# Modulation vectors of a diffusion block: VectorE multiply-adds on raw weight slabs in place of split slabs and TensorE row products

## What is computed

```
def adaln(cvec, w, b):                        # w: (1024, 6144), b: (6144,)
    m = silu(cvec) @ w + b
    return split(m, 6)                        # shift1, scale1, gate1, shift2, scale2, gate2

layer 0:  sh1, sc1, g1, sh2, sc2, g2 = adaln(c, ada_w[0], ada_b[0])        # and the same with c_ctx for t
          x += g1 * ab_mixer(rmsnorm(x) * (1 + sc1) + sh1)                 # also t
          x += g2 * swiglu(rmsnorm(x) * (1 + sc2) + sh2)                   # also t, D_FF 2816
layer 1:  the same six vectors from ada_w[1]; for t only the first two are used
          x += g1 * attention(...)            # 16 heads of two kinds, 512 keys
          x += g2 * top2_of_8_experts(...)
out = rmsnorm(x) * final_gain
```

## Time and profile before

| | |
|---|---|
| median of 3 runs | 1918.21 us (1916.23 to 1924.85) |
| profiled execution, own time | 1920.28 us |
| its span | 1918.5 us |
| mean granted TensorE clock | 0.956 |
| PE busy / DVE busy / ACT busy | 1770.2 / 1314.5 / 994.5 us |
| slabs loaded in all / of the modulation matrices | 401 split / 48 |
| moved by DMA | 426.31 MB |

### The profile page before, as it was taken

How to read it: one execution, slowest core, us unless ns; L and a number is a source line. 1 busy time by engine, 2 the same in 40 slices (tenths; PEclk the granted TensorE clock), 3 DMA queues, 4 the chain that set the end, 5 groups by cost and what they waited for, 6 DMA issues and landing times.

```text
span 1918.5 us, 23197 instructions
## 1 busy us (share of the span) xinstructions
PE 1770.2 (92%) x8673; PEld 1411.3 (74%) x8674; DVE 1314.5 (69%) x1238; ACT 994.5 (52%) x884; POOL 10.1 (1%) x24
## 2 busy tenths in 40 slices
PE   5899978999999977899769999999999999999995
PEld 2676657888888767555658888888878887888884
DVE  5536545453535555788449798889888888888896
ACT  5444324212221153544247777777777777777674
POOL 0000000000000000000000000000000000000000
PEclk9889989999999978899869999999999999999998
DMA  9446422232232222344129999999999999999992
GB/s 354 169 156 214 153 88 71 105 117 80 87 109 72 74 91 88 110 132 143 55 86 351 341 356 335 345 335 360 339 343 348 342 352 336 361 330 356 344 354 108
DMA packets 215147, 426.31 MB, mean 222 GB/s; under 512 B 8806, under 2 KB 64648, under 8 KB 215052
## 3 DMA queue, kind: packets, MB, share of 16 engines
q1 hardware_dynamic: 210178, 420.33, 63.0%
q10 hardware_dynamic: 4234, 4.57, 0.8%
q0 software_dynamic: 640, 0.04, 0.0%
HBM read 423.86 MB, written 1.05 MB: 221 GB/s over the span
## 4 chain that ended last, share of the span: by engine, by line
PE 81%; DVE 9%; ACT 5%; issue 3%; DMA 1%; SPq 1%; DVEq 0%; ACTq 0%
PE bank L478 25%; PE bank L480 24%; PE bank L479 24%; DVE lo L428 4%; ACT hi L422 3%; PE bank L1814 2%; PE bank L1853 1%; PE bank L1516 1%; DMA raw<-in_ada_w_dram 1%; PE bank L1517 1%; DVE rowmax L1278 1%; DVE mrow L1294 1%; PE bank L1887 0%; PE bank L1507 0%; PE bank L1888 0%
## 5 line engine op out<-in xcount | busy, mean ns | idle before, releaser
L428 DVE TENSOR_TENSOR lo<-raw,hi 128x2048 fp32r<-128x2048 f32 x401 | 910.8, 2282 | 301.6 <-ACT hi L422 299.8
L422 ACT ACTIVATE hi<-raw 128x2048 fp32r<-128x2048 f32 x401 | 763.9, 1910 | 495.7 <-PE bank L480 482.5
L478 PE MATMUL bank<-hi,xgh 128*128 128x512 f32 (+1 forms) x864 | 328.9, 381 | 9.9 <-DVE lo L428 6.3
L479 PE MATMUL bank<-lo,xgh 128*128 128x512 f32 (+1 forms) x864 | 325.2, 376 | 0.0
L480 PE MATMUL bank<-hi,xgl 128*128 128x512 f32 (+1 forms) x864 | 325.1, 376 | 0.0
L478 PEld LDWEIGHTS bank<-hi,xgh 128*128 128x128 f32 x864 | 163.0, 189 | 42.8 <-DVE lo L428 6.5
L480 PEld LDWEIGHTS bank<-hi,xgl 128*128 128x128 f32 x864 | 162.7, 188 | 33.0
L479 PEld LDWEIGHTS bank<-lo,xgh 128*128 128x128 f32 x864 | 162.8, 188 | 31.3
L478 PE MATMUL bank<-hi,aTh 128*128 128x512 f32 x396 | 159.1, 402 | 0.0
L480 PE MATMUL bank<-hi,aTl 128*128 128x512 f32 x396 | 154.8, 391 | 0.0
L479 PE MATMUL bank<-lo,aTh 128*128 128x512 f32 x396 | 154.3, 390 | 0.0
(11 more groups left out here) (315 smaller groups left out, 2314.2 us busy)
## 6 DMA issues: line engine op xcount, KB each, us to landing
raw<-in_moe_w_gate_dram SPq DMA_DIRECT2D x99, 1024.0 KB, 5.5
raw<-in_moe_w_up_dram SPq DMA_DIRECT2D x99, 1024.0 KB, 5.6
raw<-in_moe_w_down_dram SPq DMA_DIRECT2D x99, 1024.0 KB, 5.5
raw<-in_ada_w_dram SPq DMA_DIRECT2D x48, 1024.0 KB, 6.1
raw<-in_ffn_w_gate_dram SPq DMA_DIRECT2D x11, 1024.0 KB, 5.3
raw<-in_ffn_w_up_dram SPq DMA_DIRECT2D x11, 1024.0 KB, 5.5
raw<-in_ffn_w_down_dram SPq DMA_DIRECT2D x11, 1024.0 KB, 6.1
raw<-in_ab_w_in_dram SPq DMA_DIRECT2D x6, 1024.0 KB, 6.4
```

The costliest lines, as they stand in the source:

```text
L422: nc.scalar.activation(hi[n0 % SPL][:, 0:size], raw[slot][:, 0:size], ACT.Copy).then_inc(hi_ready, 1)
L428: nc.vector.tensor_tensor(lo[n0 % SPL][:, 0:size], raw[slot][:, 0:size], hi[n0 % SPL][:, 0:size].bitcast(F32), ALU.subtract).then_inc(lo_r ...
L478: nc.tensor.matmul(dst, lh, rh, start=first, stop=False, skip_group_check=True)
L479: nc.tensor.matmul(dst, lh, rl, start=False, stop=False, skip_group_check=True)
```

## The change

Blocks 0 to 3 of layer 0 stay as they were. The other 20 blocks (40 slabs) are no longer split. DVE reads the raw slab itself: for each of its 4 pieces and each conditioning vector it does one `scalar_tensor_tensor` of 128x512 (weights times a per-partition number, plus the sum so far) into `acc`; the bias lies in partition 0 of a cleared tile `biased`, which SP now loads, and stands in for the sum in the first operation. Layer 1's blocks 4 to 11 have one vector; their 4 operations go in two alternating sums, added at the end of the block. TensorE then only sums over partitions (`spread`): `acc` as weight and a column of ones for a column block (8 or 4 matmuls of one column), or ones as weight and 512 columns of `acc` for a gate row. The operations on DVE are placed by `MIX_STEPS` (input projection), beside the output projection, and by `FFN_BLOCKS`: one or two blocks in each feed-forward step, whose loop is now written out. None is left in the attention. GpSimd's queue is empty.

```diff
+MIX_STEPS = [[(4, 0)], [(4, 1), (5, 0)], [(5, 1)], [(6, 0), (6, 1)], [(7, 0)], [(7, 1)]]
 for j_ in range(6):
-    MIX_SLABS += [("ab_in", j_)] + [("ada0", (4 + j_, h)) for h in range(2)]
-MIX_SLABS += [("ada0", (cb, h)) for cb in (10, 11) for h in range(2)]
-MIX_SLABS += [("ada1", (cb, h)) for cb in (0, 1) for h in range(2)]
-MIX_SLABS += [("ab_out", (h, q)) for h in range(2) for q in range(2)]
-MIX_SLABS += [("ada1", (cb, h)) for cb in (2, 3) for h in range(2)]
+    MIX_SLABS += [("ab_in", j_)] + [("ada0", key) for key in MIX_STEPS[j_]]
+for h_ in range(2):
+    MIX_SLABS += [("ab_out", (h_, q)) for q in range(2)] + [("ada0", (8 + h_, q)) for q in range(2)]
+FFN_BLOCKS = [[]] + [[(0, 10)], [(0, 11)], [(1, 0)], [(1, 1)], [(1, 2)], [(1, 3)], [(1, 6), (1, 7)], [(1, 8), (1, 9)],
+                     [(1, 4), (1, 5)], [(1, 10), (1, 11)]]
...
+            def direct(layer, cb, h):
...
+                ops = [(k, who, who) for k in range(4) for who in range(2)] if pair else [(k, 0, k % 2) for k in range(4)]
+                for i, (k, who, part) in enumerate(ops):
+                    w_, c_ = raw[slot][:, 512 * k:512 * k + 512], cs[:, 8 * who + 4 * h + k:8 * who + 4 * h + k + 1]
+                    sum_ = acc[:, place_, part, :]
+                    if i >= 2 or h:
+                        chain.wait(1 if i else 0)
...
+                        ins = V.scalar_tensor_tensor(out=sum_, in0=w_, scalar=c_,
+                                                     in1=biased[:, place_, :] if h == 0 and i < 2 else sum_,
+                                                     op0=ALU.mult, op1=ALU.add)
...
             for j in range(6):
                 project("ab_in", [(j, 256)], 8, range(4), tok(Hhi, Hlo), lambda t: (j, t), None if j else h_ready[0])
-                rows_of_block(0, 4 + j)
-                if j >= 1:
-                    columns_of(0, 3 + j)
...
+                if j in (2, 3):
+                    spread(0, 2 + j)
...
+                for layer, cb in FFN_BLOCKS[i]:
+                    for h in range(2):
+                        direct(layer, cb, h)
+                hidden(i, i % 2)
...
+                    if b_ == 0 and kind == "g" and i >= 2:
+                        for layer, cb in FFN_BLOCKS[i - 1]:
+                            spread(layer, cb)
...
-                if i % 4 == 0 and i >= 4:
-                    columns_of(1, late_block(i - 4))
-                if i < 32 and i % 2 == 0:
-                    rows_of(1, late_block(i - i % 4), i % 4 // 2)
```

More of the change, by code:

```diff
@@ L97, in bank_order @@
     out.append(("start", 1, [("cT", 0)]))
[L98 to L101, removed]
+    for cb in range(4):
+        out.append(("ada0", 1, [(("m", cb), 5 + cb % 2, (cb, 1)), (("col", cb), 7)]))
+    out.append(("ada0", 1, [(("bc", cb, who), 5 + who) for cb in (4, 5) for who in range(2)] + [(("col", cb), b) for cb, b in ((6, 7), (7, 5), (8, 6), (9, 7))]))
     out.append(("norm0", 1, [(k, k % 5) for k in range(8)]))
@@ L207, in mark, with wait @@
         self.n += 1
[L209 to L218, removed]
+    def wait(self, back=0):
+        self.eng.wait_ge(self.sem, self.n - back)
 def build(nc, a, out):
-    slabs, n, landed = {}, 0, [0] * RAW
+    slabs, splits_made, directs_made, landed, held = {}, 0, 0, [0] * RAW, []
     for stage, times, keys in slab_order():
@@ L616, in _ @@
             load(sp, "ukv", 0, columns(a["d_w_ukv"][0], slice(0, 2), 0, D))
-            for cb in LATE:
-                for h in range(2):
-                    ada(1, (cb, h))
             for h in range(2):
@@ L834, in _ @@
                             "uq", (h, a_))
-            for stage, key in LATE_SLABS[0:2]:
-                splits(stage, key)
+            splits(*LAST_SLABS[0])
             for t in range(NT):
@@ L1053, in _ @@
                         emptied(V.tensor_copy(zp[:, t, (j - 4) * 256:(j - 3) * 256], b[:, 0:256]), "ab_in", (j, t))
-                mix(3 * j + 3, 3 * j + 6)
-                mod_row(0, 4 + j)
-                if j >= 1 and 3 + j not in GATE_BLOCKS:
-                    mod_col(0, 3 + j)
+                if j < 5:
+                    splits("ab_in", j + 1)
+                for cb, h in MIX_STEPS[j]:
+                    direct(0, cb, h)
                 if j == 3:
@@ L1506, in columns_of @@
                 for j in range(4):
[L1507 removed]
+                    for who in range(2 if in_pair(layer, cb) else 1):
+                        ins = T.matmul(b[:, 2 * j + who:2 * j + who + 1], sums[:, who, j * P:(j + 1) * P], ones[:, 0:1],
+                                       start=True, stop=True)
                 filled(ins, st, ("col", cb))
[L1510 to L1522 removed]
             def norm(i):
@@ L1666, in _ @@
-            hidden("u", "ffn_out", "u9", 9)
-            down("ffn_out", "d8", 8, 0)
-            hidden("g", "ffn_out", "g10", 10)
-            hidden("u", "ffn_out", "u10", 10)
-            down("ffn_out", "d9", 9, 1)
-            down("ffn_out", "d10", 10, 0)
+            hidden("g", 0)
+            hidden("u", 0)
+            hidden("g", 1)
+            for i in range(1, FFI):
+                hidden("u", i)
+                down(i - 1)
+                if i + 1 < FFI:
+                    hidden("g", i + 1)
@@ L1673, in _ @@
+            down(FFI - 1)
+            for layer, cb in FFN_BLOCKS[FFI - 1]:
+                spread(layer, cb)
             norm(2)
```

498 lines of the change are left out of this document (238 added, 260 removed).

## The result

| | before | changed kernel |
|---|---|---|
| median | 1920.13 us (1916.23 to 1924.85, 4 runs) | 1878.57 us (1875.79 to 1881.64, 4 runs) |
| ratio of the two | | 0.978, 95% interval 0.977 to 0.980 |
| profiled execution / its span | 1920.28 / 1918.5 us | 1878.65 / 1876.4 us |
| mean granted clock | 0.956 | 0.937 |
| PE / DVE / ACT busy | 1770.2 / 1314.5 / 994.5 us | 1727.8 / 1389.2 / 920.6 us |

The account below looks back on a forecast made before the run. TensorE was taken as the only bound of the feed-forward part, other stages as mixed. From 1920.3 us, -62.5 before that part, +18.4 in it, -39.5 attention and -0.5 rest sum to -84.1: 1836.2, forecast 1835, range 1820 to 1864.

Parts of the forecast that it names:

- The multiply-add, 0.67 us apiece: DVE's new operation on raw slabs: 0.67 us each back to back, 0.78 if fully serial; eight per two-vector slab, 5.4 us.
- The half rate of the rival: Rival: multiply-adds with two float32 SBUF sources take 1.34 us each, giving 1907 us in all; chance 0.04.
- Start and input projection: From the start to the pooling: two fewer DVE splits, -4.4 us, and no row products, -36.7 us.
- the new wait: Input projection: TensorE idles 5.6 us before gate block 5, whose banks wait for ACT's copies of block 4.
- Gating to the feed-forward part: From pooling through output projection to the feed-forward part: row blocks and small products go, -23.9 us.
- the 2.5 us of half clock that I gave back: Allowance of +2.5 us before the feed-forward part for half clock after TensorE's idle time.
- Feed-forward part: TensorE is the bound, so every added small product counts, +18.4 us; DVE's multiply-adds hide.
- Attention: Turns without slab work take 2.34 us, two turns 4.7 instead of 7.6, in 15 pairs: -39.5 us.
- two turns run at half clock, +4: Attention: TensorE's idle time puts only two turns at half clock, costing 4 us of the gain.
- the rival of half clock: Rival: without row products the whole attention runs at half clock, 4.7 us a turn, 1901 us in all; chance 0.04.
- Expert stage: Taken as untouched by the change and unchanged in time: 0 us.
- Rest: Table `ones` loaded in the start instead of before the routing, -0.5 us; removed GpSimd bias loads, 0.

Follow-up runs that it names:

- kd_first: Changed kernel with the attention's 96-row heads before its 64-row heads, same instructions and number: 1847.7 us, ratio 0.963.
- gate_only: Changed kernel with ACT evacuating gate block 4 ahead of the last Gelu in the input projection: 1869.1 us, ratio 0.975.
- shift96: Changed kernel with 96 instructions that do nothing in TensorE's queue ahead of the expert loop: 1856.3 us, ratio 0.968.
- shift16: Changed kernel with 16 already fulfilled waits in TensorE's queue ahead of the expert loop: 1856.6 us, ratio 0.967.
- early: Changed kernel, ACT evacuating gate block 4 ahead of the last Gelu and VectorE splitting slab 5 ahead of slab 4's copies: 1866.1 us, ratio 0.972.
- before_shift160: Kernel before the change with 160 already fulfilled waits in TensorE's queue ahead of the expert loop: 1940.0 us, ratio 1.011.
- shift240: Changed kernel with 240 already fulfilled waits in TensorE's queue ahead of the expert loop: 1880.0 us, ratio 0.979.

## Why the prediction was half right

By its own steps:

- **The multiply-add, 0.67 us apiece: right.** Of `acc<-raw,cs,acc` and `acc<-raw,cs,biased` by form, count | busy, mean ns | idle:

```profile
L1023 DVE SCALAR_TENSOR_TENSOR acc<-raw,cs,acc 128x512 f32<-128x512 f32 x216 | 146.5, 745 | 1.4
...
L1023 DVE SCALAR_TENSOR_TENSOR acc<-raw,cs,biased 128x512 f32<-128x512 f32 x32 | 22.9, 746 | 1.4 <-PE bank L1509 1.4
```

  Eight take 5.38 us. The half rate of the rival, and of the Trainium skill's rule (Vector Engine (DVE) Microarchitecture Reference, "Points that are easy to get wrong"), does not show: 216 of them beside DMA writes last 745 ns on average, as in the earlier trace rows.
- **Start and input projection: right, step for step.** TensorE starts at 55.23 (forecast 55.3), the new wait is 5.62 (5.6), the second 2.72 (2.9), VectorE ends last with two slabs of multiply-adds and two splits, gating at 150.7 (151.6), pooling at 151.99 (152.7):

```profile
141.03 5.38 DVE L1023 SCALAR_TENSOR_TENSOR acc<-raw,cs,acc 128x512 f32<-128x512 f32 x8
146.32 4.48 DVE L463 TENSOR_TENSOR lo<-raw,hi 128x2048 fp32r<-128x2048 f32 x2
150.73 1.38 DVE L1077 SCALAR_TENSOR_TENSOR u<-bank,pcols,u 128x128 f32<-128x128 f32 x5
```

  Chance had a share in it: kernels with the same instructions there begin the feed-forward part between 228.8 and 233.4.
- **Gating to the feed-forward part: right, up to here 6.7 better.** 15.6, 48.2 and 14.7 us instead of 17.5, 48.3 and 16, and the 2.5 us of half clock that I gave back were hardly there.
- **Feed-forward part: +14.9 instead of +18.4.** TensorE is the bound and clock 1.00 holds, so every small product counts, as forecast. A column block takes less than the one before, from which I had scaled, and two gate rows 1.88 instead of 2.1:

```profile
293.47 1.88 PE L1509 MATMUL bank<-acc,ones 128*128 128x512 f32 x4
363.38 1.84 PE L1515 MATMUL bank<-ones,acc 128*128 128x1 f32 x16
```

- **Attention: this step failed**, -12.8 for -39.5. The words that failed are "two turns run at half clock, +4". The pace at full clock was right (2.33 us, VectorE not in the way; `kd_first` takes 90.0 us, the forecast was 91.4), but the whole 64-row half ran at half clock: 13 turns at 4.75 us cost 13 x 2.4 = 31 us where 4 were given. My turn of 2.34 came from the half with 96-row heads. In the other half the clock had come up, in the kernel before, behind the first eight row products of 128 rows and 512 columns, and just these the change took away:

```profile
794.68 0.59 PE L1516 MATMUL bank<-hi,C 128*4 128x512 f32 x1
...
797.63 0.63 PE L1517 MATMUL bank<-lo,C 128*4 128x512 f32 x1
798.18 1.14 PE L1744 MATMUL bank<-kcT,qcT 64*128 64x512 f32 x2
```

  The score product of 64 rows behind them takes 1.14 us, and the one ahead of them 2.04. That the row products raised the clock is read from this place; no run put them back alone. I had weighed the rival of half clock at 0.04, because 32 transposes had raised the clock; I never asked what the score product of the first 16 units looks like. The rival's price, twice 2.34 for a turn, was right for half of the stage. The Trainium skill's rule on it (TensorE: Matmul & The Clock Gate, "PE-mode transpose") points the right way in a mixture full of transposes. It does not say what decided here: with the same transposes, more rows in the score product brought the clock back.
- **Expert stage: failed as well**, +21.0 for 0. "The change touches nothing in it" was true of its work and false of the place of its instructions. 50% of the missing gain lies there, and nothing in the profile of before spoke of it except three waits named "issue" of 1.5, 1.3 and 0.9 us, which I had passed over.
- **Rest: +4.0 for -0.5**: 2.3 between the feed-forward part and the attention and 1.8 behind the attention, where TensorE's granted clock is 0.73 instead of 0.76. With the same instructions the first of these stretches takes 126.6 us in the changed kernel and 126.9 in `gate_only`, but 124.1 to 124.4 in `shift96`, `shift16` and `kd_first` (before: 124.3), so this is the scatter of single executions.

The range was too narrow for two misses at once: with the attention's alone the time would have been 1862 by these terms, inside it (`shift96` has 1856.3).

## What to carry to other kernels

Products that seem to be overhead can be what brings TensorE's clock up. Before taking them out, look at every kind of product that stays, its rows above all, and at what stands where the clock has to rise. Another order of the work, or zeros beside narrow operands, brought the clock back here at almost no cost. In a loop that is not unrolled, look for "issue" waits behind the first products of a turn: an edit ahead of it can move its first instruction to a bad place, and a few empty instructions move it away (16 were enough here); compare two kernels only after looking at this. And a wait on TensorE costs more than its length where idle time brings the clock down, and is handed on to the engine that then seems to be the bound.

## What the runs showed of the hardware that was not expected

- Instructions reach the engines over a DMA queue of their own, in pieces of 16 KB (1.25 MB in 76 packets). The four shifts fit a piece of 256 instructions: 96 more brought the changed kernel's loop to the place modulo 256 of the kernel before, 160 more did the opposite, and 240, which is 16 less, put the stall eight products later. The queue's row in the changed kernel, packets, MB and share of the DMA engines' time:

```profile
q8 instruction: 76, 1.25, 0.3%
```

  At a jump back TensorE waits 0.7 to 1.5 us (once 2.7, in `shift16`, and once 3.1, in `early`) ahead of the turn's first product. Where a stall follows, it ends some 5 us after that product (4.9 to 5.6), with the slab loads at a DMA share of 0.92. In the feed-forward part, which has no loop in the changed kernel, no such wait shows (383.79 us busy of 383.79). That the fetch competes with the slab loads was not tried.
- With TensorE busy without a gap for 66 us, 64-row score products among 64-column values and transposes left the clock at 0.50; 96 rows, or 128 of which 64 were zero, raised it within one to four turns; once up, it held with 64 rows. That was tried for this mixture only.
- An instruction that only waits for something long fulfilled costs TensorE's queue, by estimate, 60 to 100 ns: it stood 5.1 us at 80 of them (`before_shift160`), and 9.1 and 11.4 us at 120 (`shift240`).
